# First MLP in two phases, modulation in the projection, last down products tile by tile earlier

## The reference

```python
for i in range(2):                                   # first block
    sh1, sc1, g1, sh2, sc2, g2 = split(silu(c) @ ada_w[i] + ada_b[i], 6)      # modulation
    u = layer_norm(h) * (1 + sc1) + sh1
    y = (concat(conv_mixer(u @ w_in), sub_ln(diff_attention(u @ w_in))) @ w_out_mix if i == 0
         else fourier_mix(u) @ w_out_fourier)
    h = layer_norm_affine(alpha * h + g1 * y, ln_g[i, 0], ln_b[i, 0])
    u = layer_norm(h) * (1 + sc2) + sh2
    h = layer_norm_affine(alpha * h + g2 * (square(relu(u @ mlp_w1[i])) @ mlp_w2[i]), ln_g[i, 1], ln_b[i, 1])
# second block: in_2, pool / conformer / RG-LRU mixers, out_2, then
h = h + square(relu(rmsnorm(h) @ w_up)) @ w_down
return rmsnorm(h)
```

## Time and profile before

| | |
|---|---|
| median of 3 runs | 3121.57 us (3121.11 to 3122.23) |
| span of the profiled execution | 3123.9 us |
| PE busy | 3016.0 us, 97% |
| DVE busy | 2237.8 us, 72% |
| ACT, POOL busy | 1309.7 us, 638.9 us |
| mlp0 on PE, first to last matmul | 668.1 to 1355.4 us |
| mlp1 on PE | 1531.0 to 2165.2 us |

### The profile page before, as it was taken

The page is one execution under the profiler, slowest core; times in us unless marked ns, Lnnn a source line. Parts: engine busy times, 40 slices in busy tenths (PEclk is TensorE's granted clock), DMA queues, the critical chain, the costliest instruction groups (busy, mean ns, idle before and its releaser), DMA issues. The chain is left out here.

```text
span 3123.9 us, 36049 instructions
## 1 busy us (share of the span) xinstructions
PE 3016.0 (97%) x14139; PEld 2476.2 (79%) x14139; DVE 2237.8 (72%) x2938; ACT 1309.7 (42%) x1963; POOL 638.9 (20%) x567
## 2 busy tenths in 40 slices
PE   6999999999999999999999999999898999999998
PEld 2888888878888888878788877887777788888887
DVE  4716488586677777585787788787697777778575
ACT  4411387363333333342643333337427553333334
POOL 0010335244344434040421120002000112120000
PEclk9999999999999999999999999999999999999999
DMA  7426321212332232211144475432111225457432
GB/s 242 145 84 212 86 80 55 99 48 83 100 101 82 95 103 99 75 37 48 68 164 149 149 282 206 149 101 69 41 55 55 95 98 182 149 197 281 172 102 101
DMA packets 213843, 369.94 MB, mean 118 GB/s; under 512 B 14599, under 2 KB 125818, under 8 KB 213674
## 3 DMA queue, kind: packets, MB, share of 16 engines
q1 hardware_dynamic: 176474, 240.02, 23.5%
q0 software_dynamic: 28848, 97.21, 8.3%
q10 hardware_dynamic: 8352, 30.41, 2.7%
HBM read 284.75 MB, written 82.84 MB: 118 GB/s over the span
## 5 line engine op out<-in xcount | busy, mean ns | idle before, releaser
L687 PE MATMUL psum<-U_hi,page_r 128*128 128x512 f32 x1660 | 656.6, 396 | 24.3 <-DVE U_lo L698 12.9
L688 PE MATMUL psum<-U_lo,page_r 128*128 128x512 f32 x1660 | 648.1, 390 | 0.0
L689 PE MATMUL psum<-U_hi,page_r 128*128 128x512 f32 x1660 | 647.8, 390 | 0.0
L687 PE MATMUL psum<-page_r,act_page_r 128*128 128x512 f32 x1272 | 496.1, 390 | 4.7 <-DVE page_r L698 4.7
L688 PE MATMUL psum<-page_r,act_page_r 128*128 128x512 f32 x1272 | 495.4, 389 | 0.0
L689 PE MATMUL psum<-page_r,act_page_r 128*128 128x512 f32 x1216 | 473.7, 390 | 0.0
L698 DVE TENSOR_TENSOR page_r<-page,page_r 128x1024 fp32r<-128x1024 f32 (+1 forms) x184 | 233.9, 1276 | 249.9 <-ACT page_r L693 245.0
L687 PEld LDWEIGHTS psum<-U_hi,page_r 128*128 128x128 f32 x1660 | 312.6, 188 | 102.1 <-DVE U_lo L698 21.4
L689 PEld LDWEIGHTS psum<-U_hi,page_r 128*128 128x128 f32 x1660 | 312.6, 188 | 66.4
L688 PEld LDWEIGHTS psum<-U_lo,page_r 128*128 128x128 f32 x1660 | 312.9, 189 | 62.2
L693 ACT CAST page_r<-page 128x1024 fp32r<-128x1024 f32 (+1 forms) x218 | 214.7, 989 | 318.1 <-PE psum L689 125.9
(11 more groups left out here) (417 smaller groups left out, 5444.1 us busy)
## 6 DMA issues: line engine op xcount, KB each, us to landing
d_act_mlp<-page POOLq DMA_DIRECT2D x222, 256.0 KB, 3.8
act_land<-d_act_mlp SPq DMA_DIRECT2D x108, 512.0 KB, 3.7
page<-in_mlp_w_dram SPq DMA_DIRECT2D x68, 512.0 KB, 4.3
page<-in_ada_w_dram SPq DMA_DIRECT2D x48, 512.0 KB, 4.8
page<-in_w_in_dram SPq DMA_DIRECT2D x38, 512.0 KB, 4.1
pair_raw<-in_mlp_w_dram SPq DMA_DIRECT2D x14, 1024.0 KB, 5.6
pair_raw<-in_w_up_dram SPq DMA_DIRECT2D x14, 1024.0 KB, 5.4
ada_land<-in_ada_w_dram ACTq DMA_DIRECT2D x24, 512.0 KB, 4.7
```

Of the source, the lines that this page charges most:

```text
L687: pe.matmul(out, l_hi, r_hi, start=start, stop=False, skip_group_check=read_between)
L688: pe.matmul(out, l_hi, r_lo, start=False, stop=False, skip_group_check=read_between)
L689: return pe.matmul(out, l_lo, r_hi, start=False, stop=stop, skip_group_check=read_between)
```

## The change

It does four things.

1. mlp0 takes the form of mlp1 and mlp2 (TWO_PHASE). The block form, its gate products on POOL and the loads of ada_w beside it are removed. The end of mlp0 and post1 get an order of their own on ACT and DVE (act_fold_seam, dve_fold_seam), in which post1's mean and square of the early tiles lie behind the last down products on ACT (act_stats, which replaces the square where the boundary is no rms norm). Row tiles are taken in FOLD_ORDER from post0 on.
2. All 96 units of ada_w are loaded in the projection. The 72 which are left there stand beside the convolution units as ADA_BESIDE_CONV says, 24 beside the first. Three sums on PE come among the V tiles, six after convolution tiles; the modulation of each part is written by DVE inside the adding of a later one (MOD_AT).
3. BY_TILE_FROM: in the last down product of mlp0 and mlp2 only step 0 is done for all tiles, and steps 1 to 3 tile by tile; mlp1 keeps steps 2 and 3. In mlp0 the gate row (1, 0) is turned inside the last product.
4. The Fourier stage takes its tiles from the new places (folded_tile), and POOL makes two of its sums.

The diff, cut to its core:

```diff
-TWO_PHASE = ("mlp1", "mlp2")
-GATE_OF = {"mlp1": (1, 1)}
+TWO_PHASE = ("mlp0", "mlp1", "mlp2")
+GATE_OF = {"mlp0": (0, 1), "mlp1": (1, 1)}
...
         for part in (1, 2, 0):
             up(w_in, part * D_CONV + i * P)
-            ada_units(2)
+            ada_units(ADA_BESIDE_CONV[3 * i + (1, 2, 0).index(part)])
...
+ADA_BESIDE_CONV = (24, 6, 5, 4, 5, 4, 4, 4, 4, 4, 4, 4)
+ADA_SUM_AFTER_V = {3: (0, 3), 6: (0, 4), 9: (0, 5)}
+ADA_SUM_AFTER_CONV = {1: (1, 0), 2: (1, 1), 3: (1, 2), 5: (1, 3), 6: (1, 4), 10: (1, 5)}
+MOD_AT = 5
...
         m.then_inc(*k.up_done.inc("v", t))
+        if t in ADA_SUM_AFTER_V:
+            pe_ada_sum(k, pe, on, *ADA_SUM_AFTER_V[t])
...
-            if m in (2, 6):
-                pe_ada_sum(k, pe, on, 0, 3 + m // 6, (k.row_b, k.row_g)[m // 6])
-    pe_ada_sum(k, pe, on, 0, 5, k.row_b)
+            if m in ADA_SUM_AFTER_CONV:
+                pe_ada_sum(k, pe, on, *ADA_SUM_AFTER_CONV[m])
...
+BY_TILE_FROM = {"mlp0": 1, "mlp1": 2, "mlp2": 1}
...
-    for d in range(2 if last else STEPS_OF):
+    by_tile = BY_TILE_FROM[name]
+    for d in range(by_tile if last else STEPS_OF):
         for t in range(TPC):
             m = part(d, t)
...
     if last:
         for t in range(TPC):
-            for d in range(2, STEPS_OF):
+            if after and after.fourier and t == 1:
+                pe_gate_row(k, pe, on, 1, 0, CHAIN_BANKS[2:])
+            for d in range(by_tile, STEPS_OF):
                 m = part(d, t)
...
+def dve_fold_seam(k, dve, on, name, b):
+    measure = lambda which, t: dve_norm_measure(k, dve, on, b, which, t)
+    scale = lambda which, t: dve_norm_scale(k, dve, on, b, which, t)
+    def post(n):
+        dve_down_add(k, dve, on, name, len(DOWN_ORDER) - 1, n - TPC)
+        measure("post", n)
+    at = k.first["table"]
+    scale("pre", TPC - 1)
+    dve_weights(k, dve, on, at)
+    dve_odd_fold(k, dve, on, 0)
+    post(4)
+    dve_odd_low(k, dve, on, 0)
+    dve_odd_fold(k, dve, on, 1)
+    scale("post", 4)
+    post(5)
+    dve_odd_low(k, dve, on, 1)
+    scale("post", 5)
+    dve_weights(k, dve, on, at + 1)
+    post(6)
+    scale("post", 6)
+    measure("pre", 4)
+    scale("pre", 4)
+    post(7)
+    scale("post", 7)
+    dve_gain(k, dve, on, b, 7)
+    measure("pre", 5)
+    scale("pre", 5)
+    measure("pre", 7)
+    dve_odd_fold(k, dve, on, 2)
+    measure("pre", 6)
+    scale("pre", 6)
+    scale("pre", 7)
+    dve_odd_low(k, dve, on, 2)
+    dve_odd_fold(k, dve, on, 3)
...
-    pe_mlp(k, pe, on, "mlp0", BOUNDARY[0], BOUNDARY[1])
+    pe_two_phase(k, pe, on, "mlp0", BOUNDARY[0], BOUNDARY[1])
```

More of the change, by code:

```diff
@@ L397, in ada_units, with mlp @@
             del ada[:n]
[L399 to L414, removed]
+        def mlp(name, w1, w2):
+            for j in range(FB):
+                up(w1, j * P)
+                units[-1].spot = (name, j)
+            units.append(Unit([], two_phase=(name, w1, w2)))
         ada_units(2 * KT)
@@ L488, in plan_units @@
         self.units, self.split, self.beside = units, [], {}
[L489 to L492, removed]
-        order, blk_first = {}, {}
+        assert not ada
+        order = {}
         for n, u in enumerate(units):
@@ L1033, in dve_turn_chunk @@
             between(i)
-STASHED = {"post2": "mlp1", "pre4": "mlp2"}
+STASHED = {"post0": "mlp0", "post2": "mlp1", "pre4": "mlp2"}
 def stash_of(k, c, i):
@@ L1046, in stash_free @@
     else:
-        on.wait_ge(*k.pe_done.at("even", KT - 1))
+        if stage == "post0":
+            on.wait_ge(*k.lo.at("u", "heads", NCH - 1, HEADS - 1))
+        else:
+            on.wait_ge(*k.pe_done.at("even", KT - 1))
         if c:
@@ L1812, in behind @@
     def behind(self):
-        return self.down[0] if self.down[0] in TWO_PHASE else None
+        return self.down if self.down in TWO_PHASE else None
     def by_pool(self, tt):
-        return tt in self.order[:self.on_pool] and not (self.behind and tt < TPC)
+        return tt < self.on_pool and not (self.behind and tt < TPC)
     @property
@@ L2075, in dve_norm_measure @@
     else:
-        on.wait_ge(*k.h_added.at(b.down, t, 1))
-    dve_measure(k, dve, on, k.H[:, t, :], P, D, b.rms if which == "pre" else False, b.name, which, t)
+        on.wait_ge(*b.added(k, t))
+    dve_measure(k, dve, on, b.h(k, t), P, D, b.rms if which == "pre" else False, b.name, which, t)
 def dve_norm_scale(k, dve, on, b, which, t):
@@ L3414, in dve_two_phase @@
                 gate("17"[i - 5], 1, d)
+        if name == "mlp0" and i == FIRST_DONE - 1:
+            dve_gate_row(k, dve, on, 1, 0)
+    if after and after.fourier:
+        dve_fold_seam(k, dve, on, name, after)
+        return
     if after:
@@ L3449, in pool_two_phase @@
         if n > PLAIN:
-            for what in ("12",) + sums:
+            store("12", n - 1)
+            store("S1", n - 1)
+        if n > PLAIN:
+            for what in sums[1:]:
                 store(what, n - 1)
```

704 lines of the change are left out of this document (158 added, 546 removed).

## The result

The changed kernel takes 3145.92 us in the median of 4 runs (3138.64 to 3147.39), the kernel before on the same chip 3121.9 (3121.11 to 3126.33). The ratio is 1.0065, 95% interval 1.005 to 1.008: it is slower, where 3108 us and a gain were forecast, and it lies above the range of 3092 to 3124. The same kernel measured again, with 12 runs of the kernel before beside it, gave 1.0057 (1.0042 to 1.0072).

The account below looks back on a forecast made before the run. PE was taken as the bound, busy 3016.0 of 3123.9 us. Terms -42.0 + 2.5 - 2.8 + 1.0 + 10.2 + 16 + 1.5 = -13.6 gave 3110.3, less 2.3 to the median: 3108 us, range 3092 to 3124.

Parts of the forecast that it names:

- the +16 for the late loads: Projection: PE's sums wait for ada_w loads that come late through the three-page ring, 16 us more.
- the +1.5 for slow matmuls: Projection: matmuls run slow after three waits of PE for late loads, 1.5 us more in all.
- rival 1: Projection: the load ring keeps up at 1.63 us a load, no wait left; 3090 us, 3099 if half holds; chance 0.22.
- The formula: Projection: loads ready at 176.3 + 74 p, so PE's waits are about 74 p - 139.6 us; p is time per load.
- the list of what differs between the new mlp0 and mlp1: mlp0: mlp1's 634.2 us adjusted by -4.1, +1.0, +4.4 and +1.0, plus 8.7 of waiting before, gives 645.2 us.
- The first tile: Start of mlp0: PE waits 8.7 us for PSUM bank 1 until DVE's add to H frees it.
- The last product: mlp0, tile by tile from step 1: waits of 3.6 us for weight 54 and 1.0 more for weight 55; +4.4 taken.
- the +2.5 for the seam: mlp0 to Fourier: DVE's queue makes the third odd fold ready 23 us after the last product, for 20.2: +2.5 us.
- The entry of mlp1: First matmul of mlp1: its 4.24 us bank wait ends, low parts of U next late by about 1.4: -2.8 us.
- mlp2: Last product by tile from step 1: PE waits for weight 54's low part, +1 us, between 0 and +3.
- Rival 3: Seams cost more: each further tile ahead of the odd folds costs some 4 us on DVE; 3115 to 3125; chance 0.20.
- Rival 4: Projection: the load ring becomes the bound, waits over 29.6 us at a landing of 5.5 us and more; chance 0.07.

Follow-up runs that it names:

- e_noload: Changed kernel without 42 of the 48 loads of layer 1's ada_w and DVE's additions of them, sums on PE kept: 3115.53 us.
- ctrl: The changed kernel measured again with nothing edited: 3142.46 us.
- e_ring5: Changed kernel with five raw pages in the ring for loads beside the convolution tiles, in place of three: 3115.17 us.
- e_back: Changed kernel with SP loading H back for mlp0 in the order of DVE's adds, in place of by number: 3135.96 us.
- e_pool: Changed kernel with GpSimd's two sums of folds after mlp0 made by DVE after the last odd fold: 3139.82 us.
- e_tile: Changed kernel with the last down product of mlp0 and mlp2 tile by tile from step 2 on, in place of step 1: 3137.98 us.

## Why the prediction was wrong

**Matmuls: right.** 192 fewer, 28.0 us less busy time even with the six sums and the slow matmuls in it.

**Projection: 27.7 forecast, 36.5 measured. The failing terms are the +16 for the late loads and the +1.5 for slow matmuls, 17.5 together for 25.4.** The sums are right (10.2; the runs without waits show 11.1). PE's waits add up to 15.9 us, in three places, the largest after tile 6, and rival 1 is refuted: the landings in this stretch are 3.4 us at the shortest and 4.7 in the median. In the Trainium skill ("DMA: Bandwidth & Descriptors", "Anatomy of one DMA") the 2.0 us and 436 GB/s that the prediction quotes are given for DMAs that GpSimd issues; these are SP's.

That the waits match the +16 is luck. The formula gives by how much the loads are behind PE at the sum after tile 6, and what fills this time is waits and slow matmuls together. Without the loads PE is there at 315.51, in e_noload:

```profile
315.51 1.84 PE L722 MATMUL psum<-ones,row_g 128*128 128x1 f32 x16
```

In the changed kernel it is 337.12, and with the starts of the two projections (59.96 and 59.37) taken off that is 22.2 us later, for the 16 that I took; another 3.2 come after it. So ctrl's projection is as long with shorter waits: its sum stands at 337.53, when the loads are there, and more of the time before it went to slow matmuls.

The loads were later than the formula says for a reason that it doesn't have. It lets them run through from 176.3 on. They did start a little earlier (172.46), but between 222.23 and 232.60 none starts. DVE has added the first 24 by 222.2 and comes to the low part of a convolution weight, whose hi part isn't there. ACT makes it only at 230.17, behind a copy of a V tile for which it waits for PE:

```profile
220.92 1.29 DVE L711 SCALAR_TENSOR_TENSOR row_b<-page,cc,row_b 128x1024 f32<-128x1024 f32 x1 [1.62 <-DMA page<-in_ada_w_dram]
231.35 1.22 DVE L658 TENSOR_TENSOR page_r<-page,page_r 128x1024 fp32r<-128x1024 f32 x1 [9.14 <-ACT page_r L653]
```

The same wait had ended at 229.55 in the kernel before; I had read it as room for loads and not as a place where the ring stops. From 231.35 on, 49 units are done by 337.06, 2.16 us each, near the 2.13 of the prediction; over the pause it is 2.26. The second of the three waits ends with DVE's gate product of the convolution, which stands behind an addition that waited 1.86 us for its load.

What follows a wait I mis-sized too. I took 0.5 us for each of three waits. But here a wait is followed by 16 small matmuls, and they stretch as well: the sum at 270.00 takes 3.58 us for 1.84, then matmuls come at 0.43 us for 0.23 until 278.7. The windows show the granted clock:

```profile
260.00:280.00 20.00, 15.98 (x61) 13.24 (x60) 10.95 (x13) 3.07 (x4) 0.00 (x0) 0.74 0.83 260
330.00:345.00 15.00, 7.88 (x29) 6.99 (x30) 8.57 (x10) 2.02 (x3) 1.08 (x2) 0.54 0.86 285
```

(columns as in the earlier trace rows; the clock is the third number from the end). 0.74 and 0.54 where it was 1.00 all through before. After the wait of 9.12 us that ends at 337 the clock is at the lower of its two levels (1.2 GHz of 2.4) as the matmuls start again. Together the slow matmuls are 9.5 us, six times the term. That the waits and this cost go with the ring of three pages is shown by e_ring5.

**mlp0: -50.8 forecast from first to last matmul, -41.8 measured. The failing step is the list of what differs between the new mlp0 and mlp1, which puts one difference at nothing without a reason:** the four pairs of loads of H on SP's queue, in an order by number, against DVE's adds in FOLD_ORDER. I had taken mlp1's time as it stood and looked for what differs only on PE, DVE and ACT; the changed order of tiles was in the diff, and SP's loads by number were in the code that the diff doesn't touch. mlp1's own time has a wait of 2.42 us at this place, so 6.6 of the 9.01 us are new, and some 2 us of slow matmuls behind them. e_back shows it: with the loads in order the stage takes 637.4 us, for 636.5 in my sum.

**The first tile: right,** 8.41 us for 8.7. The profile names no releaser, but DVE's add to H ends at 712.02 and PE starts at 712.12. I did not see that any other start of the ring, taken alone, moves the wait to mlp1.

**The last product: the wait right in size, wrong in what it is worth.** 3.65 us for 3.6. The further 1.0 us for weight 55 did not come, and didn't follow from the rows: after the wait, step 3 is wanted at 2149.3 + 1.4 = 2150.7, and the low part is there at 2150.5. With step 2 in its place the seam takes half of the saving back.

**Seam and Fourier: -0.3 forecast, +7.5 measured. The failing term is the +2.5 for the seam.** The entry of mlp1 did lose its 4.24 us; 1.8 of it come back inside mlp1 (636.0 for 634.2), for the 1.4 that I had allowed. But the third odd fold comes 32.0 us after the end of mlp0 (1389.56 - 1357.54), for 20.2 before and 23 in my sum. "Over 28 us" stood among the prediction's signs of being wrong. I had summed DVE's passes by their lengths alone. On DVE's and GpSimd's timelines of the changed kernel:

```profile
1352.27 1.17 DVE L658 TENSOR_TENSOR odd_fold_lo<-fold_temp,odd_fold_hi 128x1024 fp32r<-128x1024 f32 x1
...
1357.31 3.38 DVE L658 TENSOR_TENSOR odd_fold_lo<-fold_temp,odd_fold_hi 128x1024 fp32r<-128x1024 f32 x1
...
1362.93 2.83 DVE L658 TENSOR_TENSOR page_r<-page,page_r 128x512 fp32r<-128x512 f32 x1 [1.92 <-ACT page_r L653]
...
1373.62 2.31 DVE L1996 SCALAR_TENSOR_TENSOR H<-H,small,row_g 128x1024 f32<-128x1024 f32 x1
1375.97 3.29 DVE L1998 SCALAR_TENSOR_TENSOR H<-H,small,row_b 128x1024 f32<-128x1024 f32 x1
```

```profile
1357.22 2.38 POOL L2203 TENSOR_TENSOR H<-H,row_g 128x1024 f32<-128x1024 f32 x1 [321.21 <-ACT H L1896]
1359.69 3.23 POOL L2205 TENSOR_TENSOR H<-H,row_b 128x1024 f32<-128x1024 f32 x1
...
1374.81 6.66 POOL L3157 TENSOR_TENSOR XF<-XF 128x1024 f32<-128x1024 f32 x2
```

The same low part takes 1.17 us alone and 3.38 beside GpSimd; four passes are longer by 2.2, 2.1, 1.0 and 2.0 us, 7.3 in all. e_pool shows it for the last of them; for the other three it is read from the timeline and wasn't tried by itself. Besides, DVE stands 1.9 us for the table's hi part on ACT, five times 0.36 us and once 1.55 for roots, 5.3 together. The stretch and these waits are more than the 9.0 us that were missing; how much of the waits my hand sum already held, the prediction doesn't show. By the Trainium skill ("GPSIMD Engine Reference", "Specifications") GpSimd shares its SBUF interfaces with VectorE, with contention where a VectorE instruction has two SBUF inputs or runs in a 2-port mode. The trace agrees: the passes with two inputs from SBUF stretch, while the measures (L794, one input) take 1.27 to 1.29 us a pair and the adds from PSUM (L2702) 0.68, beside GpSimd too. A row for it was there before the run, and I had summed with 1.2 (the kernel before, DVE's and GpSimd's timelines):

```profile
1355.68 3.14 DVE L3575 TENSOR_TENSOR fold_temp<-XF 128x1024 f32<-128x1024 f32 x1
```

```profile
1355.35 2.39 POOL L2243 TENSOR_TENSOR H<-H,row_b 128x1024 f32<-128x1024 f32 x1
```

**mlp2: right in size,** the rest of the kernel +1.0 for +1; the by-tile form gains nothing there, and without it e_tile's rest is 1.5 to 2 us shorter.

**The base and the reckoning.** I put the profiled execution of the kernel before 2.3 us above the median. In fact a run's time is its span and 1.7 to 1.9 us more for that kernel, and 2.1 to 2.2 for the changed one, so that execution was one of some 3125.7 us, and the forecast from its span would have been 3110.3 + 2.1 = 3112.4. That is 4.4 us of the 37.9 between 3108 and 3145.9. The profiled execution of the changed kernel was the fastest of its four, 7.3 under their median. What is left is 26.2 between the spans (3110.3 and 3136.5): 8.8 in the projection, 0.7 up to mlp0, 8.9 in mlp0, 9.6 in the seam, Fourier and mlp1, less 1.9 of an earlier start. Each was small against the range; all three large ones went the same way, since each was a cost left out.

Rival 3, "the seams cost more", had the seam's size: DVE's chain some 9 us longer, though by stretched passes and waits for ACT and not by more tiles. Rival 4, "slower than before", had the verdict, at a chance of 0.07, and the ring as the cause; but the landing stayed at 4.7 us and not 5.5, the ring's share is 25.4 us and not over 29.6, and without the 8.9 and 9.6 us of mlp0 and the seam the span would have been shorter than before, not 12.6 us longer.

## What to carry to other kernels

When a stage is rebuilt by the pattern of another, compare every queue of the two, SP's loads among them, in the order in which their tiles are wanted; a list by number and a list by place agree only by luck. Where work moves to a ring of buffers, landing and use over the number of pages is only the best pace it can have (1.44 us for a measured 2.0 with five pages here); look also for places where the ring stands still because the engine that empties it waits for something else. Still count the pages first: two more were worth 27 us, and each other order of the same work under 9. Where a chain of loads decides when PE may go on, the cost is by how much it is late; waits and slow matmuls before that point share it and don't add to it. After the last wait the lower clock does add.

## What the runs showed that I had not expected

- With three waits of 15.9 us the projection is 25.4 us longer, since large and small matmuls stretch after them (a sum takes 3.58 us for 1.84); with 13.0 us of waits it is just as long.
- The place at which a ring of PSUM banks starts in one stage sets the waits two stages on: the same 8.41 us stood at the entry of mlp0 or of mlp1, and neither once both starts were chosen.
- With five loads in flight a load of 512 KB lands in 5.9 us for 4.7 with three, and more comes in all the same, one every 2.0 us for 2.4.
- A pass of DVE with two inputs from SBUF takes up to 3.4 us for 1.2 beside a pass of GpSimd.
